# Second gated feed-forward of a two-block model: down projection in rounded parts, inner tiles in groups of 8, 8 and 6

## The reference

```python
def swiglu(h, w_in, w_out):
    a, u = jnp.split(h @ w_in, 2, axis=-1)
    return (jax.nn.silu(a) * u) @ w_out
...
        h = h + gt1_l * y_l
        h = h + gt2_l * swiglu(modulate(rms_norm_2(h, norm_ffn_w[i]), sh2_l, sc2_l), ffn_w_in[i], ffn_w_out[i])
        if not last:
            hc = hc + gt1_c * y_c
            hc = hc + gt2_c * swiglu(modulate(rms_norm_2(hc, norm_ffn_w[i]), sh2_c, sc2_c),
                                     ffn_w_in[i], ffn_w_out[i])
```

## Time and profile before

| | |
|---|---|
| median of three runs | 3512.0 us (3511.22 to 3512.82) |
| profiled execution | 3522.42 us |
| its span | 3520.6 us |
| granted TensorE clock, mean over the span | 0.953 |
| TensorE busy | 3207.3 us, 91% |
| VectorE busy | 1557.3 us, 44% |
| ScalarE busy | 1149.3 us, 33% |
| GpSimd busy | 581.6 us, 17% |
| HBM read | 261 MB, mean 75 GB/s |

### The profile page before, as it was taken

The page is one execution under the profiler, slowest core; times in us unless marked ns, Lnnn a source line. Parts: engine busy times, 40 slices in busy tenths (PEclk is TensorE's granted clock), DMA queues, the critical chain, the costliest instruction groups (busy, mean ns, idle before and its releaser), DMA issues. The chain is left out here.

```text
span 3520.6 us, 49050 instructions
## 1 busy us (share of the span) xinstructions
PE 3207.3 (91%) x19218; PEld 2423.0 (69%) x19218; DVE 1557.3 (44%) x2402; ACT 1149.3 (33%) x1754; POOL 581.6 (17%) x490
## 2 busy tenths in 40 slices
PE   7988877998898899989787899999989999899998
PEld 5665631576665688767676788885548888648877
DVE  5644288233424566333665322220026788533332
ACT  4212253142203332234576322210024455223321
POOL 0000021000102344141354300000032222100001
PEclk9999988999999999989999899999989999899999
DMA  3575100121231122221000111111122111112212
GB/s 129 194 255 193 69 31 0 72 85 61 82 122 48 72 95 88 83 87 39 35 2 1 48 48 71 71 41 50 50 78 72 58 70 55 72 66 101 96 66 90
DMA packets 30571, 267.95 MB, mean 76 GB/s; under 512 B 2864, under 2 KB 5296, under 8 KB 10160
## 3 DMA queue, kind: packets, MB, share of 16 engines
q1 hardware_dynamic: 30384, 265.36, 20.5%
HBM read 261.15 MB, written 4.19 MB: 75 GB/s over the span
## 5 line engine op out<-in xcount | busy, mean ns | idle before, releaser
L633 PE MATMUL banks<-normed_high,weights_high 128*128 128x512 f32 (+1 forms) x2328 | 870.5, 381 | 92.6 <-DVEq L455 50.3
L633 PE MATMUL banks<-normed_low,weights_high 128*128 128x512 f32 (+1 forms) x2328 | 857.1, 375 | 0.0
L633 PEld LDWEIGHTS banks<-normed_high,weights_high 128*128 128x128 f32 x2328 | 449.6, 193 | 205.8 <-ACT weights_high L543 47.7
L633 PE MATMUL banks<-normed_high,weights_low 128*128 128x512 f32 (+1 forms) x2328 | 559.2, 371 | 0.0
L263 DVE TENSOR_TENSOR weights_low<-ring,weights_high 128x1024 fp32r<-128x1024 f32 (+1 forms) x202 | 279.8, 1385 | 583.1 <-ACTq L556 527.9
L633 PEld LDWEIGHTS banks<-normed_low,weights_high 128*128 128x128 f32 x2328 | 451.3, 194 | 76.8 <-issue 2.6
L554 ACT ACTIVATE weights_high<-ring 128x1024 fp32r<-128x1024 f32 (+1 forms) x233 | 268.3, 1151 | 643.6 <-PE banks L633 475.0
L633 PEld LDWEIGHTS banks<-normed_high,weights_low 128*128 128x128 f32 x2328 | 416.6, 191 | 75.6
L588 POOL TENSOR_TENSOR latent_total<-latent_total,latent_square 128x512 f32<-128x512 f32 x42 | 78.5, 1868 | 1449.1 <-ACTq L531 1449.1
L633 PE MATMUL banks<-ffn_hidden,ring 128*128 128x256 f32 (+1 forms) x704 | 227.3, 486 | 1.1 <-PEq L154 1.1
L2875 PE MATMUL banks<-normed_high,hg_weights_high 128*128 128x512 f32 (+1 forms) x512 | 189.8, 371 | 15.1 <-DVEq L455 15.1
(11 more groups left out here) (541 smaller groups left out, 4687.2 us busy)
## 6 DMA issues: line engine op xcount, KB each, us to landing
ring<-in_ffn_up SPq DMA_DIRECT2D x33, 2048.0 KB, 7.5
ring<-in_ada SPq DMA_DIRECT2D x48, 1024.0 KB, 6.3
ring<-in_ffn_down SPq DMA_DIRECT2D x24, 1408.0 KB, 5.8
ring<-in_hgrn SPq DMA_DIRECT2D x16, 1536.0 KB, 6.3
ring<-in_gates SPq DMA_DIRECT2D x6, 2048.0 KB, 8.2
ring<-in_wo SPq DMA_DIRECT2D x6, 2048.0 KB, 8.0
ring<-in_w_rw SPq DMA_DIRECT2D x5, 1536.0 KB, 7.5
ring<-in_branch SPq DMA_DIRECT2D x3, 2048.0 KB, 8.1
```

Source lines behind the costliest of these rows:

```text
L633: mm = pe.matmul(ps[:, 0:y.shape[-1]], w, y, start=(not sweep and kk == 0 and n == 0), stop=(sweep != 0 and kk == kt - 1 and n == len(pair ...
```

## The change

The down projection of this feed-forward is now computed in rounded parts like the others. For that the hidden tensor is a `Split` of 8 tiles instead of 22 in float32, and up and down projection are cut into three groups of 8, 8 and 6 hidden tiles: up for the group, then down for the group, whose share is added to the residual. The up weights are the same slots in three sections of 4, 4 and 3; the down weights become three sections of 8 slots with 8, 8 and 6 inner tiles. The norms are made in the first up stage alone, the squares are collected in the last down stage alone. Silu and product go into a new small buffer `G`, from which `both_parts` writes the two parts.

```diff
-            ("ffn_up2", 11, 4096), ("ffn_down2", 8, FT * P), ("hgrn", 2 * DT, 3 * DT * P), ("wo3", 2, 4096),
+            ("ffn_up2a", 4, 4096), ("ffn_down2a", 8, 8 * P), ("ffn_up2b", 4, 4096), ("ffn_down2b", 8, 8 * P),
+            ("ffn_up2c", 3, 4096), ("ffn_down2c", 8, 6 * P), ("hgrn", 2 * DT, 3 * DT * P), ("wo3", 2, 4096),
...
-def both_parts(e, U, t, x):
+def both_parts(e, U, t, x, a=None, b=None):
 
-    hi, lo = at(U.hi, t), at(U.lo, t)
+    hi, lo = at(U.hi, t, a, b), at(U.lo, t, a, b)
...
-    def gated(section, rhs, layer, which, parts, kt=DT, tiles=4, back=None):
+    def gated(section, rhs, layer, which, parts, kt=DT, tiles=4, back=None, last=True):
...
-        linear(k, section, [rhs(LAT), rhs(CTX_)][:parts], add, kt=kt, tiles=tiles, sums=[latent, context][:parts])
+        linear(k, section, [rhs(LAT), rhs(CTX_)][:parts], add, kt=kt, tiles=tiles, sums=[latent, context][:parts] if last else ())
...
-    def swiglu(H, up, down, layer, parts):
+    def swiglu(H, layer, thirds):
+
         with ExitStack() as s1:
-            U = k.sb("ffn_hidden", [P, FT, T], s1)
+            U = Split(k, "ffn_hidden", T, s1, tiles=8)
+            G = k.sb("ffn_gate", [P, 2, T], s1)
 
             def act(e, t, part, ps, at_):
                 a, b = (CTX, T) if part == 0 else (0, CTX)
-                j = at_.n // parts
-                u = at(U, hidden(at_, j % 2), a, b)
+                j = at_.n // 2
+                g = G[:, j % 2, a:b]
                 if j < 2:
-                    e.eng.activation(u, ps[:, 0:b - a], ACT.Silu).then_inc(e.sem, e.tick())
+                    if at_.i is not None or at_.s > 0:
+                        e.eng.wait_ge(*at_.emptied("vector", at_.n - 4))
+                    e.eng.activation(g, ps[:, 0:b - a], ACT.Silu).then_inc(e.sem, e.tick())
                     e.eng.wait_ge(e.sem, e.now())
                     return
-                e.eng.wait_ge(*at_.emptied("scalar", at_.n - 2 * parts))
-                e.eng.tensor_tensor(u, u, ps[:, 0:b - a], ALU.mult).then_inc(e.sem, e.tick())
+                e.eng.wait_ge(*at_.emptied("scalar", at_.n - 4))
+                e.eng.tensor_tensor(g, g, ps[:, 0:b - a], ALU.mult).then_inc(e.sem, e.tick())
                 e.eng.wait_ge(e.sem, e.now())
-            linear(k, up, [H.operand(LAT), H.operand(CTX_)][:parts], act,
-                   on=["scalar", "scalar", "vector", "vector"],
-                   norms=[modulated(H.at, layer, 1, 1), modulated(H.at, layer, 1, 0)])
-            gated(down, lambda c: lambda kk: U[:, kk, c], layer, 1, parts, kt=FT, tiles=1)
+                both_parts(e, U, hidden(at_, j - 2), g, a, b)
+            for n, (up, down, tiles) in enumerate(thirds):
+                linear(k, up, [H.operand(LAT), H.operand(CTX_)], act, on=["scalar", "scalar", "vector", "vector"],
+                       per=[1, 1, 3, 3], norms=() if n else [modulated(H.at, layer, 1, 1), modulated(H.at, layer, 1, 0)])
+                gated(down, U.operand, layer, 1, 2, kt=tiles, tiles=1, last=(n == len(thirds) - 1))
...
-        swiglu(H, "ffn_up2", "ffn_down2", 0, 2)
+        swiglu(H, 0, (("ffn_up2a", "ffn_down2a", 8), ("ffn_up2b", "ffn_down2b", 8), ("ffn_up2c", "ffn_down2c", 6)))
```

More of the change, by code:

```diff
@@ L3384, in lay_out @@
         d["ffn_down" + n] = slots(a["ffn_w_out_2"][l], 1)
+    up, down = d.pop("ffn_up2"), a["ffn_w_out_2"][0]
+    d.pop("ffn_down2")
+    for n, s in (("a", 0), ("b", 4), ("c", 8)):
+        d["ffn_up2" + n], d["ffn_down2" + n] = up[s:s + 4], slots(down[2 * P * s:2 * P * (s + 4)], 1)
     h = a["hgrn_w_in_2"][0].reshape(D, 5, 8, P)[:, [2, 3, 1, 4, 0]].transpose(0, 2, 1, 3).reshape(D, 5 * D)
```

## The result

| | before | after |
|---|---|---|
| median of the runs | 3512.0 us (3511.22 to 3519.93, 5 runs) | 3487.0 us (3483.69 to 3495.8, 5 runs) |
| ratio of after to before | | 0.9931, 95% interval 0.9914 to 0.9948 |
| profiled execution, its span | 3522.42, 3520.6 us | 3487.0, 3485.1 us |
| granted clock, mean | 0.953 | 0.954 |
| first up tile to the gated recurrence's first matmul | 1998.40 to 2619.89: 621.5 us | 1992.86 to 2586.53: 593.7 us |

The change saves 25.0 us by the medians. The last row of the table is the better measure of the change itself, since it leaves out what both kernels share: **27.8 us less**. The two profiled executions differ by 35.5 us, of which 5.5 lie ahead of this stretch and 2.2 behind it, in code that is the same in both. The stretch of before is read from its one profile; that of the change came out at 593.7 us in two (experiment 6).

A forecast was written before the change was run, and what follows sets the result against it. TensorE alone was taken to bound the stretch: 43.6 us of shorter stream, less 11.8 for idle times and 8.5 for the clock, gives 23.3 us less, 3488.8 us. Range 3482 to 3496, or 3479 to 3499 with rivals and slow loads.

The forecast's parts named there:

- The stream: TensorE's down-projection matmuls: float32 tiles become rounded tiles of 8.34 and 6.26 us, making the stream 43.6 us shorter.
- No wait inside the down stages: Within the down projections, smaller weight loads (4 us assumed) and roundings stay hidden behind TensorE's tiles: cost 0.
- The idle times: TensorE idle at five new stage boundaries, 2.8, 1.6, 2.8, 1.6 and 3.5 us; 11.8 us more in all, records included.
- The 256-column cast: VectorE's cast at 256 columns in the up projection, put between 0.1 and 0.43 us and taken as 0.29.
- The clock: Granted clock falls to 1.2 GHz behind each of five boundaries, mean loss 1.7 us: 8.5 us, bounds 1 and 15.
- Rival 1: The clock hardly falls at any of the five boundaries: 30.8 us less, 3481.2 us; chance 0.15.
- Rival 2: Stage entries stall on fetching code jumped to, 0.84 us each at five entries and two loops: 6 us, 3494.7; chance 0.12.
- Rival 4: In the down stages a loop or a register wait makes tiles slower than 8.34 us; chance 0.02.
- Rival 3: Small down-weight loads land late, at 9.2 us: 33 us more, 3522 us, decisive from about 8.4 us; chance 0.03.
- The median: Whole kernel's median time: 23.3 us less subtracted from the median before of 3512.0, giving 3488.8 us.

The follow-up runs named there:

- experiment 6: The changed kernel run again, nothing altered, for a second profile: 3487.8 us, ratio 0.9917 to the kernel before.
- Experiment 5: The change with the low-weights by high-operand product left out of the down stages except for each tile's last inner tile: 3438.8 us, ratio 0.9777.
- Experiment 4: The change with another 1536 KB loaded ahead of each down slot, so that the slot's own load lands late: 3505.3 us, ratio 0.9971.
- experiment 3: The change with the down stages of the first two groups written out instead of looped: 3483.5 us, ratio 0.9911.
- experiment 1: Groups of 8, 8 and 6 as in the change, but hidden tensor and down projection left in float32: 3520.8 us, ratio 1.0014.
- the fourth group: The change cut into four groups of 6, 6, 6 and 4 hidden tiles instead of three: 3495.0 us, ratio 0.9941.
- experiment 8: The change with each next stage's first weights rounded at the end of the stage before, and the table load moved earlier: 3477.9 us, ratio 0.9897.
- experiments 9 to 11: Early weights with the first two groups' down stages written out (3488.1 us), then looped (3480.6 us) and written out again (3479.6 us) on one chip.
- early weights: The change with first weights of every stage but the first rounded one stage ahead, table load early; looped or written out: 3477.9, 3488.1, 3480.6, 3479.6 us.

## Why the prediction was right, point by point

Forecast 3488.8 us, measured 3487.0, with 23.3 us less forecast and 27.8 found in the stretch.

- **The stream: right.** Every down tile without a boundary ahead is 8.34 us in the first two groups (2154.36 to 2162.70) and 6.26 in the third (2531.50 to 2537.76); up tiles are 8.34 too. The 43.6 us hold. (The Trainium skill, TensorE: Matmul & The Clock Gate, "Back-to-back issue gap", gave 7.8 us by the prediction's estimate; neither the up nor the down tiles here agree.) Experiment 5 shows the stream as the bound from the other side.
- **No wait inside the down stages: right, with more room than thought.** Loads of 384 and 512 KB land in 3.0 and 3.3 us (median); 4 was assumed, and the range had 6.2. Experiment 4 shows what it would have cost.
- **The idle times: right.** 2.8, 1.6, 2.8, 1.6 and 3.5 were forecast, 2.82, 1.62, 2.82, 1.62 and 3.52 came. The 256-column cast, not in the trace of before, took 0.29 us. The chain of rows, put together from other boundaries, held to 0.06 us (2.79, 1.61 and 3.46 before rounding).
- **The clock: the mis-sized term.** "Five boundaries: 8.5 us" was the mean of four rows, by 5. The first tiles of the five stages took 10.08, 8.44, 8.45, 8.44 and 7.98 us; less 8.34 (6.26 for the last) that is 1.74, 0.10, 0.11, 0.10 and 1.72, 3.8 us in all. With it the prediction's own sum gives 43.6 - 11.8 - 3.8 = 28.0 us, and 27.8 were measured. The size of a fall was near (1.7 forecast, 1.7 measured); the number was not: five were priced and two came. The step that failed is that it laid one mean over idle times of different length: in the rows at hand 4.40 and 3.36 us had lost 2.2 and 3.0, 1.82 us once 1.5 and once 0.2. Two of the five idle times, 1.62 us, were shorter than any of these and lost 0.1. The third without a fall, 2.82 us at the second group, is not explained by its length, and no row of before could have told it.
- **Rival 1** (the clock hardly falls) was the nearer for this term, but two falls of 1.7 us were there. **Rival 2** (stalls of code fetching, 0.84 us each) does not show: 0.41 us lie between VectorE's end at 2142.72 and ScalarE's start, and a loop's entry adds 0.35 us, hidden in the change. (What the Trainium skill, Runtime: NRT & Kernel Launch, "Instruction fetch mechanics", says of fetches behind taken branches costs nothing at these entries that the rows show, unless the 0.35 us are such a fetch, which no run tells.) **Rival 4** is out by the tiles of 8.34 us, and by experiment 3. **Rival 3** was made to happen in experiment 4 and proved dearer than its working.
- **The median** came within 1.8 us of the forecast, partly by chance: of the 27.8 us, 25.0 stand in the medians, and 23.3 had been forecast for both. The time ahead of the stretch, in unchanged code, ran from 1985.1 to 1998.4 us over the executions profiled, so 2 to 3 us in a difference of medians are within the scatter; by its interval of 0.9914 to 0.9948 the ratio leaves room for 18 to 30 us.

## What to carry to other kernels

Cost a cut of one stage into several as a sum over boundaries, each put together from the last evacuation, the barrier, a table load and the first rounding; such a sum held here to 0.06 us each, and experiment 1 shows that the cut alone would have been a loss of 7.4 us. Behind each boundary price the clock by the length of its idle time, as a chance of losing some 1.7 us and not as a fixed cost. And before making groups smaller, compare the tile's time with the landing of the large load that is issued one tile ahead of the next stage: at 6.26 us against 7.9 the fourth group cost 12.3 us instead of some 6. The late load is 2.2 us of the difference as idle time; most of the rest is falls of the clock, two of them behind the idle times that it made longer.

## What the runs showed of the hardware

**The clock behind idle time.** Over the twelve profiles of kernels with rounded parts (the change, and all experiments but the first), TensorE's idle times in the middle of the stretch and what followed:

| idle time, us | how many | clock fell behind it |
|---|---|---|
| 0.58 to 1.76 | 21 | 0 |
| 1.83 to 2.03 | 11 | 4 |
| 2.17 to 2.90 | 33 | 23 |
| 3.41 to 3.52 | 6 | 6 |

A fall cost 1.45 to 1.75 us, whatever the idle time. The length orders the chance but doesn't decide it between 1.8 and 2.9 us: the same kernel with the same idle times fell once and then three times, and the two idle times of 2.82 us always differed (four falls of four at the first place, none of four at the second). What decides in that band stays open; it is neither the length nor the program alone.

**A stretch can be told from its boundaries.** With 577.1 us for the rest (experiment 8: 587.8 - 9.0 - 1.7), plus the idle times, plus 1.7 for each fall, experiments 9 to 11 come to 593.9, 590.1 and 586.5 us; measured were 594.2, 590.7 and 587.3.

**The fastest version** run here has early weights: medians of 3477.9, 3488.1, 3480.6 and 3479.6 us, ratios to before of 0.9897, 0.9912, 0.9901 and 0.9894, against 0.9931 and 0.9917 for the change. In the profiles it has some 3 us less of idle time. The two ran on one chip once, in experiments 6 and 8: 3487.8 us for the change (six runs, 3478.6 to 3492.5) against 3477.9 (four runs, 3474.1 to 3483.2). The means differ by 8.4 us, and by the scatter of these ten times an estimate of the 95% interval is 2 to 15 us. So early weights beat the change there; by how much is not well known.
